# First LayerNorm's gain and offset rows made on TensorE from their columns, their load dropped and its room filled early; router logits woven between output products

## The chip, the cores and the metric

The kernel runs on one NeuronCore of one Trainium2 chip. The metric is the time of one execution on the device in microseconds (us). Three executions of the kernel before gave 1113.84, 1113.93 and 1114.98 us, so the median is 1113.93 us. A difference under 0.2% (2.2 us) counts as none here.

## What is computed

The reference is one layer of a streaming encoder in float32 for 384 tokens (a prompt of 256 and 8 streams of 16), width 1024:

```
m = W_out( concat[ beta_ret * Retention(x), beta_conv * ShortConv(x) ] )
h = LayerNorm1(alpha * x + m)            # gain ln1_g, offset ln1_b
y = LayerNorm2(alpha * h + MoE(h))       # top 4 of 32 experts, clamped SwiGLU
```

Each expert has a gate-and-up matrix of 1024 x 2048 and a down matrix of 1024 x 1024, 12 MB in all. All 32 experts are read. The router's logits are a product of h with a 1024 x 32 matrix.

## The kernel before, in words

There is one instruction stream for each engine, written out by hand, with semaphores between them. The work has two stages.

The **mixer** comes first. Its weights come in 18 pieces of 1 MB. It ends with the output products (`wout`, L793 to L809): for each of three token tiles t and eight chunks c, three matmuls of 512 columns that sum into a bank. After them come transposes of h (`transpose_h`, L811), the logits (`logits`, L820, eight chunks of 32 columns in two halves), ranks of the tokens within an expert (`ranks`, L837) and the gather of the first pair's tokens (`gather_first`, L850). The list from L867 to L902 sets their order on TensorE: `wout` of tiles 0 and 1 whole, then tile 2's last four chunks woven with the transposes and logits of tiles 0 and 1, then the rest. VectorE finishes each tile meanwhile (`residual`, `row_stats`, `logit_offset`, `choose`, called from L1688 on), and ScalarE copies transposes out of the banks and normalises rows (`copy_h_t`, `norm_rows`).

The **experts** follow, two at a time (`pair`). In TensorE's stream a pair is: `gate_up(0)`, small products, `gate_up(1)`, `down(0)`, the gather of the next pair's tokens (in the first pair it comes after `down(1)`), `down(1)`. `gate_up` has eight chunks c, each 1 MB of weights, `down` eight chunks of 0.5 MB. Both take a table of things to do between chunks. When a chunk is done, TensorE raises `piece_used`.

The weights go through rooms in SBUF: a ring of 12 rooms of 1 MB and five more (`old_rooms`), and for the first four pairs some rooms aside. Among the aside rooms is `lnp` (1 MB, called `LATE[2]` as a piece: rows of the first expert's down matrix, chunks 4 and 5 of `down(0)`). All of these DMAs are issued by SyncE, strictly in order: before an issue SyncE waits until `piece_used` says that the room's last reader is through. The queue of issues is thus stopped by the oldest room that is not yet free. In the part that matters here the order is: two pieces after the last output product, `xy` (`LATE[3]`) once `h_raw` says that VectorE's residuals are done, the two `EARLY` pieces after the last logit, two rooms as `gate_up(0)` frees them, then pair 1's pieces. Within pair 1, after its first run, SyncE waits for `h_ready` and issues `LATE[2]` into `lnp` (L525 to L527).

`lnp` is late because it holds the first norm's gain and offset until then. ScalarE issues two DMAs that spread each row of 1024 numbers over 128 partitions (L1242 to L1244, 512 KB each). VectorE multiplies and adds them to the normalised rows in `gain_and_offset` (L1625 to L1632, six operations on 128 x 1024), after its part of the first pair's gathered tokens and ahead of `softmax`. The same gain and offset are also in SBUF as columns, `ln1_t`, with 8 columns each (value p + 128 c in partition p, column c).

Further up in the mixer, `first_streams` (L743) has TensorE overwrite banks that VectorE has read in its group norm. It waits on `o_free`, raised by the last of the group norm's operations (L1525). `gate_rows(0)` (L1530) comes right behind on VectorE.

Of the kernel before, what the change touches and what calls it, by code (L numbers as in the profile page):

```python
# [29 lines left out]
ALU = mybir.AluOpType  # L30
# [3 lines left out]
D = 1024  # L34
KC = D // 128
# [94 lines left out]
def build(nc, x_tok, x_t, s_ret, conv_in, w_in, w_out, chan, beta_ret, ln1, ln2, w_router, b_router,  # L130
# [3 lines left out]
    with es:  # L134
# [121 lines left out]
        with ExitStack() as gap:  # L256
# [20 lines left out]
        xt_in, x_in, cst_in, mcst_in, st_in = map(sem, ("xt_in", "x_in", "cst_in", "mcst_in", "st_in"))  # L277
        chan_in, bias_in, ln1_in, ln2_in, router_in = map(sem, ("chan_in", "bias_in", "ln1_in", "ln2_in", "router_in"))
        rows_stored, retp_stored = sem("rows_stored"), sem("retp_stored")
# [11 lines left out]
        chan_mm, c_out, u_out, conv_ready = map(sem, ("chan_mm", "c_out", "u_out", "conv_ready"))  # L291
        gn_var, gn_rstd, o_free, o_ready_m = map(sem, ("gn_var", "gn_rstd", "o_free", "o_ready_m"))
        kd_ready, stp_mm, stp_out = sem("kd_ready"), sem("stp_mm"), sem("stp_out")
# [5 lines left out]
            sem, ("wr_ready", "wr_sum_in", "wr_sum_mm", "wr_sum_out"))  # L299
        row_shift, norm_ready, h_ready = map(sem, ("row_shift", "norm_ready", "h_ready"))  # L300
        half_gathered, first_xg, first_xg_v = map(sem, ("half_gathered", "first_xg", "first_xg_v"))
        h_t, h_t_out = sem("h_t"), sem("h_t_out")
# [110 lines left out]
        def _(sp):  # L413
# [87 lines left out]
            def aside_pieces(pair, ea, eb):  # L501

                used = MIX_PIECES + (pair - 1) * PAIR_PIECES
                aside = [run for run in runs if run[0] in LATE]
                cycled = [run for run in runs if run[0] not in LATE]
                ahead = sum(unit_of[aside_fill(pair, j) + units - 1 - WIDE] < (pair - 1) * PAIR_PIECES + LATE[0]
                            for j, units in cycled)
                for j, units in cycled[:ahead] + aside + cycled[ahead:]:
                    if j == LATE[0]:
                        sp.wait_ge(piece_used, used + LATE[0] + (1 if pair == 1 else 2))  # L510
                        if pair == 1:
                            sp.wait_ge(tab_ready, 1)
                        expert_run(j, ea, eb, over_q[:, :]).then_inc(side_again[j], 16)
                    elif j == LATE[2]:
                        k = (LATE[2] - LATE[0]) * 256
                        rows = w_down[bass.ds(ea, 1), k:k + 128 * DN_RUN, :].rearrange("e (p k) n -> p e (k n)", p=128)
                        for n, dst in ((0, last_old), (1, in_lnp)):
                            sp.wait_ge(piece_used, used + LATE[n + (1 if pair == 1 else 2)] + 1)
                            sp.dma_start(dst.unsqueeze(1), rows[:, :, n * PW:(n + 1) * PW])\
                                .then_inc(side_again[LATE[n + 2]], 16)  # L520
                    else:
                        g = aside_fill(pair, j)
                        room_used(g, units)
                        expert_run(j, ea, eb, rooms(g % WIDE, units)).then_inc(slot_full[g % WIDE], 16)
                    if pair == 1 and j == 0:  # L525
                        sp.wait_ge(h_ready, NT)
                        first_side(LATE[2])  # L527

# [53 lines left out]
            sp.wait_ge(h_raw, 2 * NT)  # L582
            first_side(LATE[3])
            sp.wait_ge(logit_mm, NT)
            for j in EARLY:
# [31 lines left out]
        def _(pe):  # L617
# [125 lines left out]
            def first_streams():  # L743

                pe.wait_ge(vm_ready, 2)
                pe.wait_ge(o_free, NT)
                pe.wait_ge(stp_out, 1)
                streams(0)
                streams(1)
# [123 lines left out]
            router_sums()  # L873
            for t in range(NT - 1):
                wout(t, range(4, KC))
            transpose_h(0, 0)
            transpose_h(0, 1)
            wout(NT - 1, (4,))
            logits(0, 0)
            wout(NT - 1, (5,))  # L880
            logits(0, 1)
            transpose_h(1, 0)
            wout(NT - 1, (6,))
            transpose_h(1, 1)
            wout(NT - 1, (7,))
            logits(1, 0)
            transpose_h(2, 0)
            logits(1, 1)
            transpose_h(2, 1)
            logits(2, 0)  # L890
            pe.wait_ge(sel_ready, 1)
            gate_up_bias(0)
            early_ranks()
# [8 lines left out]
            gather_first(2, range(KC))  # L902


            def count():
# [175 lines left out]
            def pair(turn, odd=False, last=False):  # L1081
# [14 lines left out]
                if not first:  # L1096
# [3 lines left out]
                        | ({2: lambda: sums_so_far(0), 6: lambda: sums_so_far(1)} if last else {})  # L1100
                        | ({2: count_before, 6: by_expert} if first else {}))
                pe.wait_ge(act_t_ready, 2 * p + 1)
                pe.wait_ge(sel_down_ready, p + 1)
                down(0, turn, odd, {4: lambda: transpose_act(1, p, 2 if first else DN_RUN)}
                     | ({2: overflow_tables} if first else {}) | ({6: lambda: sums_so_far(2)} if last else {}))
                if not first and not last:
# [34 lines left out]
        def _(act):  # L1141
# [99 lines left out]

            act.wait_ge(piece_used, IN_PIECES + 2)  # L1242
            for n in range(2):
                act.dma_start(lnp[:, n, :], ln1[n:n + 1, :].to_broadcast([128, D])).then_inc(ln1_in, 16)  # L1244
            act_banks = ((0, 1), (3, 7), (2, 4))
# [167 lines left out]
        def _(dve):  # L1413
# [106 lines left out]
            for t in range(NT):  # L1520
                dve.wait_ge(gn_rstd, t + 1)
                for h in range(H):
                    ins = dve.tensor_scalar(qo[:, t, h * 128:(h + 1) * 128], bank[t][:, h * 128:(h + 1) * 128],
                                            gmv[:, t, h, 0:1], grs[:, t, h:h + 1], ALU.subtract, ALU.mult)
                ins.then_inc(o_free, 1)  # L1525

            def gate_rows(t):

                dve.wait_ge(o_free, t + 1)
                dve.tensor_tensor(qo[:, t, :], qo[:, t, :], gg[:, t, :], ALU.mult).then_inc(o_ready_m, 1)  # L1530
# [93 lines left out]

            def gain_and_offset():  # L1625

                dve.wait_ge(ln1_in, 32)
                for t in range(NT):
                    ins = dve.tensor_tensor(hid[:, t, :], hid[:, t, :], lnp[:, 0, :], ALU.mult)
                link(ins)  # L1630
                for t in range(NT):
                    dve.tensor_tensor(hid[:, t, :], hid[:, t, :], lnp[:, 1, :], ALU.add).then_inc(h_ready, 1)  # L1632

# [75 lines left out]
            for c in range(4, KC):  # L1709
                dve.tensor_scalar(xg[:, c, :], bank[7][:, (c - 4) * 128:(c - 3) * 128], ln1_t[:, 0, c:c + 1],  # L1710
                                  ln1_t[:, 1, c:c + 1], ALU.mult, ALU.add).then_inc(first_xg_v, 1)
            gain_and_offset()

# [93 lines left out]
            def pair(p, first=False, second=False, last=False):  # L1807
# [8 lines left out]
                for a in range(2):  # L1816
# [13 lines left out]
                    if a == 0:  # L1830
# [4 lines left out]
                        if not last:  # L1835
                            dve.wait_ge(gt_mm, p + 1)
                            slots_of(p + 1)
                    elif not last:
                        rows_of(p + 1)
                if first:  # L1840
                    tables()
                if last:

# [100 lines left out]
```

## Time and profile before

| what | value |
|---|---|
| median of three executions | 1113.93 us |
| the profiled execution, its own time | 1113.32 us |
| its span, first to last instruction | 1111.4 us |
| TensorE busy | 97% of the span |
| DMA, hardware queue of the weights | 428.68 MB, 92.9% of 16 engines' span |
| VectorE, ScalarE, GpSimd busy | 30%, 19%, 8% |
| mean granted TensorE clock | 0.994 |

The busy time of TensorE (PE) is modelled from pipelined instructions, so it overstates how full the engine is; what counts is whether it has idle time and who ended it. A float32 matmul stands as two instructions in the trace, a float32 transpose as one. PEld is TensorE's loading of weights. SPq is SyncE's sequencer, which issues DMAs. The span leaves out 1.9 us around the profiled execution.

### The profile page before, as it was taken

The page shows a single profiled execution, that of the slowest core. Times are in us where ns is not written, and L with a number is a line of the kernel's source. Part 1 is how long each engine was busy: PE and PEld are TensorE (multiplying, and loading weights), DVE is VectorE, ACT ScalarE, POOL GpSimd, SP SyncE. Part 2 cuts the span into 40 slices and gives each one's busy share as a digit, 9 for nine tenths or more (in the row PEclk, how much of TensorE's full clock was granted, in tenths as well). Part 3 has the DMA queues.
Part 4 walks back from the last instruction along what each step waited for, and adds up shares of the span by engine and source line. Part 5 has one row for each costly group of instructions (what it writes and reads, how often), then busy time and mean ns, then how long its engine had stood idle before and what let it go on. Part 6 is the DMA issues. An engine that isn't in the chain of part 4 may idle for free.

```text
span 1111.4 us, 13640 instructions
## 1 busy us (share of the span) xinstructions
PE 1073.5 (97%) x5552; PEld 544.8 (49%) x5552; DVE 328.0 (30%) x601; ACT 207.4 (19%) x361; POOL 90.2 (8%) x50
## 2 busy tenths in 40 slices
PE   9999999999999999999999999999898989898995
PEld 6889988344434343434343434343434343342532
DVE  3487764512131312121212121212131312112134
ACT  3243333120111120202020202020111111110122
POOL 4675500000000000000000000000000000000002
PEclk9999999999999999999999999999999999999998
DMA  9972589999999999999999999999999999999995
GB/s 351 325 243 76 163 331 404 364 428 407 426 429 425 428 428 428 426 424 430 429 428 429 427 429 428 429 427 428 430 428 427 429 428 428 426 430 428 428 427 204
DMA packets 56611, 436.27 MB, mean 393 GB/s; under 512 B 8128, under 2 KB 18112, under 8 KB 29088
## 3 DMA queue, kind: packets, MB, share of 16 engines
q1 hardware_dynamic: 50048, 428.68, 92.9%
q10 hardware_dynamic: 6528, 7.09, 1.9%
q8 instruction: 26, 0.43, 0.2%
q14 instruction: 9, 0.07, 0.0%
HBM read 431.78 MB, written 3.97 MB: 392 GB/s over the span
## 4 chain that ended last, share of the span: by engine, by line
PE 67%; DMA 25%; DVE 1%; issue 0%; POOL 0%; ACT 0%; POOLq 0%; SPq 0%; DVEq 0%
PE bank L1012 25%; DMA ring<-w_down 25%; PE bank L1044 18%; PE bank L944 8%; PE bank L637 5%; PE bank L1073 1%; PE bank L993 1%; PE bank L864 1%; PE bank L1075 1%; PE bank L854 1%; PE bank L1021 1%; PE bank L800 1%; PE bank L780 1%; PE bank L786 1%; PE bank L803 1%; PE bank L804 1%
## 5 line engine op out<-in xcount | busy, mean ns | idle before, releaser
L1012 PE MATMUL bank<-ring,xg 128*64 128x512 f32 x1536 | 345.3, 595 | 7.2 <-DMA ring<-w_gu 7.1
L1012 PEld LDWEIGHTS bank<-ring,xg 128*64 128x64 f32 x1536 | 105.0, 136 | 209.1 <-issue 188.0
L1044 PE MATMUL bank<-ring,act_t 128*64 128x512 f32 x672 | 151.0, 595 | 8.3 <-DMA ring<-w_down 8.3
L1012 PE MATMUL bank<-old_rooms,xg 128*64 128x512 f32 x496 | 112.3, 595 | 3.7 <-DMA old_rooms<-w_gu 3.7
L1784 DVE SCALAR_TENSOR_TENSOR oo_lo<-oo_raw,gate_s,oo_hi 128x512 fp32r<-128x512 f32 x32 | 24.0, 752 | 311.0 <-ACT oo_hi L1288 311.0
L1820 DVE TENSOR_SCALAR gate_c<-bank 128x512 f32<-128x512 f32 x32 | 22.1, 691 | 249.8 <-PE bank L1012 249.8
L944 PEld LDWEIGHTS bank<-onehot,hid 128*128 128x128 f32 x720 | 85.9, 196 | 12.2 <-issue 12.2
L1044 PEld LDWEIGHTS bank<-ring,act_t 128*64 128x64 f32 x672 | 46.1, 137 | 92.8 <-issue 78.0
L944 PE MATMUL bank<-onehot,hid 128*128 128x128 f32 x720 | 88.8, 283 | 0.0
L1798 DVE TENSOR_TENSOR xy<-xy,bank 128x512 f32<-128x512 f32 x84 | 52.7, 683 | 107.6 <-PE bank L1075 107.6
L1380 POOL TENSOR_TENSOR rstd<-veps,minus_half 128x1 f32<-128x1 f32 x6 | 3.3, 545 | 961.7 <-DVE veps L1580 961.4
L1363 POOL TENSOR_TENSOR w_parts<-ring,w_parts 128x1024 fp32r<-128x1024 f32 x27 | 74.5, 2764 | 52.8 <-ACT w_parts L1159 52.8
L1012 PEld LDWEIGHTS bank<-old_rooms,xg 128*64 128x64 f32 x496 | 34.2, 136 | 66.7 <-issue 57.6
L1315 ACT COPY oo_raw<-bank 64x512 f32<-64x512 f32 x63 | 36.6, 581 | 159.9 <-PE bank L1044 159.1
L1044 PE MATMUL bank<-old_rooms,act_t 128*64 128x512 f32 x256 | 60.0, 609 | 3.8 <-DMA old_rooms<-w_down 3.8
L1299 ACT ACTIVATE sig<-gate_c 128x512 f32<-128x512 f32 x32 | 20.2, 630 | 177.6 <-DVE gate_c L1820 177.6
L1301 ACT COPY act_t<-bank 128x512 f32<-128x512 f32 x32 | 18.8, 586 | 167.0 <-PE bank L993 167.0
L1277 ACT CAST gt<-bank 128x384 fp32r<-128x384 f32 x16 | 7.7, 479 | 201.2 <-PE bank L956 201.2
L637 PE MATMUL bank<-w_parts,x_hi 128*128 128x512 f32 x180 | 44.8, 395 | 0.3 <-ACT w_parts L1159 0.3
L1159 ACT CAST w_parts<-ring 128x1024 fp32r<-128x1024 f32 x27 | 28.4, 1053 | 65.9 <-PE bank L637 60.3
L1073 PE MATMUL bank<-oo_hi,gt 128*128 128x512 f32 x90 | 38.6, 429 | 0.0
L637 PEld LDWEIGHTS bank<-w_parts,x_hi 128*128 128x128 f32 x180 | 33.6, 187 | 9.5 <-issue 1.5
(258 smaller groups left out, 942.9 us busy)
## 6 DMA issues: line engine op xcount, KB each, us to landing
ring<-w_gu SPq DMA_DIRECT2D x90, 2048.0 KB, 30.0
ring<-w_down SPq DMA_DIRECT2D x41, 2048.0 KB, 33.0
old_rooms<-w_gu SPq DMA_DIRECT2D x30, 2048.0 KB, 28.6
old_rooms<-w_down SPq DMA_DIRECT2D x18, 1024.0 KB, 24.8
old_rooms<-w_down SPq DMA_DIRECT2D x7, 2048.0 KB, 30.5
ring<-w_in SPq DMA_DIRECT2D x13, 1024.0 KB, 14.5
ring<-w_gu SPq DMA_DIRECT2D x12, 1024.0 KB, 6.9
over_q<-w_down SPq DMA_DIRECT2D x3, 2048.0 KB, 15.2
```

What stands on the lines that cost most here:

```text
L637: mm = pe.matmul(out, lhs, rhs, start=(n == 0 and c == 0), stop=(n == 2 and c == KC - 1))
L944: mm = pe.matmul(bank[6 + c // 4][:, (c % 4) * 128:(c % 4 + 1) * 128], hid[:, t, :].rearrange("p (q m k) -> p q k m", m=128, k=GU_RUN) [:, ...
L1012: mm = pe.matmul(bank[2 * a + n][64 * hf:64 * hf + 64, :], xg[:, c, 64 * a:64 * a + 64], w[:, col:col + 512], start=False, stop=(c == KC - 1))
L1044: mm = pe.matmul(bank[b][64 * hf:64 * hf + 64, :], act_t[:, a, c % 4, 64 * (c // 4):64 * (c // 4) + 64], w[:, c % run, hf * 512:(hf + 1) * ...
L1073: pe.matmul(bank[comb_banks[i]][:, :], gt[:, t * 128:(t + 1) * 128], oo_hi[:, hf, :], start=True, stop=False)
L1159: act.copy(w_parts[:, n % PARTS, 0, :], w).then_inc(w_hi_ready, 1)
L1299: act.activation(sig[:, :], gate_c[:, :], ACT.Sigmoid, scale=SIG).then_inc(sig_ready, 1)
L1315: act.copy(oo_raw[64 * a:64 * a + 64, hf, :], bank[down_banks[a]][64 * hf:64 * hf + 64, :]).then_inc(out_ready, 1)
L1363: pool.tensor_tensor(w_parts[:, n % PARTS, 1, :], w, w_parts[:, n % PARTS, 0, :].bitcast(F32), ALU.subtract).then_inc(w_lo_ready, 1)
L1784: dve.scalar_tensor_tensor(oo_lo[:, hf, :], oo_raw[:, hf, :], gate_s[:, 0:1], oo_hi[:, hf, :].bitcast(F32), ALU.mult, ALU.subtract).then_i ...
L1798: dve.tensor_tensor(xy[:, t, o], xy[:, t, o], bank[comb_banks[i]][:, :], ALU.add)\
L1820: dve.tensor_scalar(gate_c[:, :], bank[2 * a][:, :], LIMIT, None, ALU.min).then_inc(gate_ready, 1)
```

## The change

1. ScalarE no longer issues the two loads of the gain and offset rows. `ln1_rows(n)` on TensorE makes them: eight matmuls into banks 0 and 1, each with one column of `ln1_t`, repeated 128 times, as the stationary operand and the identity as the moving one. `ln1_rows(0)` (gain) stands before chunk 1 of the first pair's `gate_up(1)` and waits for `up_ready`; `ln1_rows(1)` (offset) stands before chunk 6 of its `down(0)` and waits until VectorE has used the gain.
2. VectorE's `gain_and_offset` becomes `rows_with`, called twice, with the banks as the second operand: the gain after `slots_of(1)` in the first pair, the offset after `tables`.
3. `LATE[2]` is issued right behind `LATE[3]`; the wait for `h_ready` inside pair 1 goes.
4. The order of the output products, transposes and logits is woven tighter.
5. `o_free` goes; `first_streams` waits for the first `gate_rows` instead.

```diff
-                    if pair == 1 and j == 0:
-                        sp.wait_ge(h_ready, NT)
-                        first_side(LATE[2])
...
             sp.wait_ge(h_raw, 2 * NT)
             first_side(LATE[3])
+            first_side(LATE[2])
             sp.wait_ge(logit_mm, NT)
...
-                pe.wait_ge(o_free, NT)
+                pe.wait_ge(o_ready_m, 1)
...
             router_sums()
-            for t in range(NT - 1):
-                wout(t, range(4, KC))
+            wout(0, range(4, KC))
             transpose_h(0, 0)
+            wout(1, (4, 5))
             transpose_h(0, 1)
-            wout(NT - 1, (4,))
+            wout(1, (6,))
             logits(0, 0)
-            wout(NT - 1, (5,))
+            wout(1, (7,))
             logits(0, 1)
+            wout(2, (4,))
             transpose_h(1, 0)
-            wout(NT - 1, (6,))
+            wout(2, (5,))
             transpose_h(1, 1)
-            wout(NT - 1, (7,))
+            wout(2, (6,))
             logits(1, 0)
+            wout(2, (7,))
+            logits(1, 1)
             transpose_h(2, 0)
-            logits(1, 1)
+            pe.wait_ge(sel_ready, 1)
+            gate_up_bias(0)
             transpose_h(2, 1)
             logits(2, 0)
-            pe.wait_ge(sel_ready, 1)
-            gate_up_bias(0)
             early_ranks()
             logits(2, 1)
...
+            def ln1_rows(n):
+
+                if n == 0:
+                    pe.wait_ge(up_ready, 1)
+                else:
+                    pe.wait_ge(ln1_used, NT)
+                for c in range(KC):
+                    mm = pe.matmul(bank[c // 4][:, (c % 4) * 128:(c % 4 + 1) * 128],
+                                   ln1_t[:, n, c:c + 1].to_broadcast([128, 128]), ident, start=True, stop=True)
+                mm.then_inc(ln1_mm, 1)
...
-                        | ({2: count_before, 6: by_expert} if first else {}))
+                        | ({1: lambda: ln1_rows(0), 2: count_before, 6: by_expert} if first else {}))
...
-                     | ({2: overflow_tables} if first else {}) | ({6: lambda: sums_so_far(2)} if last else {}))
+                     | ({2: overflow_tables, 6: lambda: ln1_rows(1)} if first else {}) | ({6: lambda: sums_so_far(2)} if last else {}))
...
-            act.wait_ge(piece_used, IN_PIECES + 2)
-            for n in range(2):
-                act.dma_start(lnp[:, n, :], ln1[n:n + 1, :].to_broadcast([128, D])).then_inc(ln1_in, 16)
...
-                ins.then_inc(o_free, 1)
+            link(ins)
...
-            def gain_and_offset():
-
-                dve.wait_ge(ln1_in, 32)
+            def rows_with(n, op, done):
+
+                dve.wait_ge(ln1_mm, n + 1)
                 for t in range(NT):
-                    ins = dve.tensor_tensor(hid[:, t, :], hid[:, t, :], lnp[:, 0, :], ALU.mult)
-                link(ins)
-                for t in range(NT):
-                    dve.tensor_tensor(hid[:, t, :], hid[:, t, :], lnp[:, 1, :], ALU.add).then_inc(h_ready, 1)
+                    dve.tensor_tensor(hid[:, t, :].rearrange("p (b n) -> p b n", b=2),
+                                      hid[:, t, :].rearrange("p (b n) -> p b n", b=2), banks[:, 0:2, :], op)\
+                        .then_inc(done, 1)
...
-            gain_and_offset()
...
+                        if first:
+                            rows_with(0, ALU.mult, ln1_used)
...
                 if first:
                     tables()
+                    dve.wait_ge(ln1_used, NT)
+                    rows_with(1, ALU.add, h_ready)
```

## Rows read from the trace of the kernel before

**Rows 1.** The page: busy time by engine, and what the DMAs moved in 40 slices

```profile
PE 1073.5 (97%) x5552; PEld 544.8 (49%) x5552; DVE 328.0 (30%) x601; ACT 207.4 (19%) x361; POOL 90.2 (8%) x50
...
GB/s 351 325 243 76 163 331 404 364 428 407 426 429 425 428 428 428 426 424 430 429 428 429 427 429 428 429 427 428 430 428 427 429 428 428 426 430 428 428 427 204
```

**Rows 2.** Busy time by stretch: from:to length, engines, clock, DMA share, GB/s

```profile
194.00:198.00 4.00, 4.00 (x21) 1.43 (x22) 3.82 (x7) 0.78 (x3) 0.00 (x0) 1.00 0.34 94
...
254.50:256.50 2.00, 2.00 (x12) 0.65 (x10) 0.00 (x0) 0.00 (x0) 0.00 (x0) 1.00 0.92 279
256.50:300.00 43.50, 43.50 (x231) 20.20 (x229) 9.92 (x18) 5.45 (x11) 0.00 (x0) 1.00 1.00 424
...
640.00:1090.00 450.00, 426.92 (x2152) 181.49 (x2154) 92.61 (x158) 63.80 (x118) 0.00 (x0) 1.00 1.01 428
```

**Rows 3.** SyncE's queue in order of time: start, us, what is issued

```profile
186.41 0.80 SPq L479 DMA_DIRECT2D early_rooms<-w_gu  x2
...
202.50 0.33 SPq L483 DMA_DIRECT2D lnp<-w_down  x1
...
254.66 3.76 SPq L494 DMA_DIRECT2D ring<-w_down  x2
```

**Rows 4.** What SyncE's queue waited for, 186 to 256 us: total, times, longest

```profile
SPq L494 <- PE bank L1012: 9.5, 1, 9.5
```

**Rows 5.** TensorE in order of time, pair 1's start and a late pair

```profile
251.01 7.04 PE L1012 MATMUL bank<-ring,xg 128*64 128x512 f32 x32
257.97 0.50 PE L1073 MATMUL bank<-oo_hi,gt 128*128 128x512 f32 x1
...
667.20 3.65 PE L1044 MATMUL bank<-old_rooms,act_t 128*64 128x512 f32 x16 [0.73 <-DMA old_rooms<-w_down]
```

**Rows 6.** TensorE: the first full gather, and eight transposes

```profile
244.70 5.92 PE L944 MATMUL bank<-onehot,hid 128*128 128x128 f32 x48
...
173.81 1.03 PE L814 MATMUL bank<-cst,hid 128*128 128x128 f32 x8
```

**Rows 7.** DMA issues by line: KB each, median us to landing

```profile
lnp<-ln ACTq DMA_DIRECT2D x4, 512.0 KB, 6.8
```

**Rows 8.** VectorE in order of time, first pair; idle before it in brackets

```profile
208.60 0.68 DVE L1821 TENSOR_SCALAR up_c<-bank 128x512 f32<-128x512 f32 x1
...
225.83 0.69 DVE L1820 TENSOR_SCALAR gate_c<-bank 128x512 f32<-128x512 f32 x1 [9.27 <-PE bank L1012]
...
246.29 0.75 DVE L1784 SCALAR_TENSOR_TENSOR oo_lo<-oo_raw,gate_s,oo_hi 128x512 fp32r<-128x512 f32 x1 [15.85 <-ACT oo_hi L1288]
```

**Rows 9.** The page's groups: a VectorE operation that reads a bank

```profile
L1798 DVE TENSOR_TENSOR xy<-xy,bank 128x512 f32<-128x512 f32 x84 | 52.7, 683 | 107.6 <-PE bank L1075 107.6
```

**Rows 10.** In order of time: the first gate_rows on VectorE, first streams on TensorE

```profile
115.79 2.22 DVE L1530 TENSOR_TENSOR qo<-qo,gg 128x512 f32<-128x512 f32 x1
...
117.99 1.15 PE L739 MATMUL bank<-tmp,kk 32*128 32x256 f32 x16
```

**Rows 11.** TensorE in order of time, from the ranks to the first gate_up

```profile
184.38 0.41 PE L841 MATMUL bank<-vv,cst 128*128 128x32 f32 x2 [0.22 <-DVE vv L1649]
...
186.19 4.55 PE L854 MATMUL bank<-onehot,hid 128*128 128x128 f32 x26
...
191.16 2.90 PE L854 MATMUL bank<-onehot,hid 128*128 128x128 f32 x22
```

**Rows 12.** By stretch: TensorE's clock is the third number from the end

```profile
230.10:233.50 3.40, 3.40 (x9) 0.63 (x6) 0.35 (x3) 0.00 (x0) 0.00 (x0) 0.50 1.04 443
182.30:185.70 3.40, 3.18 (x29) 2.66 (x27) 2.55 (x14) 2.87 (x5) 0.51 (x1) 1.00 1.00 407
185.70:189.10 3.40, 3.40 (x17) 3.40 (x17) 2.15 (x11) 2.57 (x5) 0.00 (x0) 0.50 1.04 439
```

**Rows 13.** TensorE in order of time, down(0) of the first pair

```profile
229.89 3.53 PE L1044 MATMUL bank<-old_rooms,act_t 128*64 128x512 f32 x8
...
234.03 1.94 PE L1044 MATMUL bank<-lnp,act_t 128*64 128x512 f32 x8
```

More of the change, by code:

```diff
@@ L277, in build @@
         xt_in, x_in, cst_in, mcst_in, st_in = map(sem, ("xt_in", "x_in", "cst_in", "mcst_in", "st_in"))
-        chan_in, bias_in, ln1_in, ln2_in, router_in = map(sem, ("chan_in", "bias_in", "ln1_in", "ln2_in", "router_in"))
+        chan_in, bias_in, ln2_in, router_in = map(sem, ("chan_in", "bias_in", "ln2_in", "router_in"))
         rows_stored, retp_stored = sem("rows_stored"), sem("retp_stored")
@@ L291, in build @@
         chan_mm, c_out, u_out, conv_ready = map(sem, ("chan_mm", "c_out", "u_out", "conv_ready"))
-        gn_var, gn_rstd, o_free, o_ready_m = map(sem, ("gn_var", "gn_rstd", "o_free", "o_ready_m"))
+        gn_var, gn_rstd, o_ready_m = map(sem, ("gn_var", "gn_rstd", "o_ready_m"))
         kd_ready, stp_mm, stp_out = sem("kd_ready"), sem("stp_mm"), sem("stp_out")
@@ L300, in build @@
         row_shift, norm_ready, h_ready = map(sem, ("row_shift", "norm_ready", "h_ready"))
+        ln1_mm, ln1_used = sem("ln1_mm"), sem("ln1_used")
         half_gathered, first_xg, first_xg_v = map(sem, ("half_gathered", "first_xg", "first_xg_v"))
@@ L1524, in _ @@
                                             gmv[:, t, h, 0:1], grs[:, t, h:h + 1], ALU.subtract, ALU.mult)
-                ins.then_inc(o_free, 1)
+            link(ins)
             def gate_rows(t):
-                dve.wait_ge(o_free, t + 1)
                 dve.tensor_tensor(qo[:, t, :], qo[:, t, :], gg[:, t, :], ALU.mult).then_inc(o_ready_m, 1)
```

## The prediction, made before the changed kernel was run

> **What bounds the kernel now.** I read the page first. TensorE is busy 97% of the span, and in the slices the DMAs move about 428 GB/s from some 170 us on, almost to the end [rows 1]. Two resources are nearly full, so I asked in which stretch each sets the pace.
>
> The table of stretches answers. From 640 to 1090 us the DMAs carry 428 GB/s without a pause, while TensorE has 23 us of idle time in 450 [rows 2]. The order of time shows what ends that idle time: a landing of expert weights [rows 5]. So the stream of weights sets the end. It runs without a gap from 256.5 us on: 424 GB/s up to 300, and the slices show no dip after that [rows 1, 2].
>
> What matters is therefore when the stream last had a gap, and who ended it. Between 254.5 and 256.5 us it moved only 279 GB/s [rows 2]. SyncE's queue issued the next transfer at 254.66 us [rows 3], after a wait of 9.5 us for TensorE's line 1012 [rows 4]. That line is the first `gate_up` of pair 1, 32 instructions from 251.01 us, four chunks [rows 5]. Two of them take half of 7 us, which gives 254.5. All rooms were full, and TensorE had to free one. **From there on the stream follows TensorE's progress at 254.66 us**, and what lies behind is the same number of bytes at the same rate. An earlier gap, 194 to 198 us at 94 GB/s [rows 2], is of the same kind and is made good by the later one: whatever the stream gains or loses before 254.66 us only changes how long it stands there.
>
> TensorE has no idle time from 186 us to 254.66 us, and 0.22 us just before that stretch [rows 11]. So the end moves with the sum of TensorE's work and waits up to 254.66 us. The one limit is the gap's own length: at 279 in place of 428 GB/s over 2 us the stream lost 0.7 us there. If TensorE came earlier by more than that, plus what the DMAs gain, the stream would be the limit.
>
> **Bytes.** The two removed loads are 512 KB each [rows 7], 1.05 MB together, and at 428 GB/s worth 2.45 us of stream. `LATE[2]`, issued at 202.50 us before [rows 3], moves about 20 us earlier, behind `LATE[3]`; its 1.05 MB now go ahead of the gap at 194 us, for which TensorE has to free nothing. The `EARLY` pieces behind it in the queue (issued at 186.41 us [rows 3]) land up to 2.45 us later, at about 198 us, since the stream's gap at 194 us says that all had landed by then. They are chunks 6 and 7 of `gate_up(0)`, which begins at 194 us behind the first gather [rows 11]; six chunks of 1.75 us [rows 5] make 204 us: nobody waits. The wait for `h_ready` goes from SyncE's queue, and with it at most the few tenths by which `LATE[2]` followed the piece before it. All this puts the stream 2.45 us ahead at 254.66 us. It stands still there 2.45 us longer. Value: 0.
>
> **New matmuls.** `ln1_rows` is called twice, eight matmuls each, 16 float32 matmuls of 128 columns with 128 columns of weights, so 32 instructions. The nearest row is a gather with the same shapes: 48 instructions from 244.70 us, 5.92 us, 0.122 us each [rows 6]. I take 32 x 0.122 = **3.9 us**. Nothing hides them: TensorE is in order and has no idle time there. From below, eight transposes of the same tile size took 1.03 us, 0.13 us each with one instruction each [rows 6]; if a matmul with a repeated column cost no more than one of these, 16 would be 2.1 us. From above, 0.132 us an instruction as in the 22 of the first gather [rows 11], which gives 4.2 us. That the column is repeated by a step of zero has no row; I see no reason for a gain or a loss in it.
>
> The Trainium skill, "Perfetto Trace Analysis", section "Optimizing Tensor Performance", asks that a logical transpose be made as a transpose and not as a standard matmul. The trace agrees: one instruction in place of two [rows 6]. By it the new rows would cost 2.1 us and not 3.9, but the change uses the matmul.
>
> **Waits that the new matmuls bring to TensorE.** `ln1_rows(0)` waits for `up_ready`, raised by an operation of 0.68 us from 208.60 us [rows 8], so at 209.3 us. It stands one chunk of 1.75 us into `gate_up(1)`, and `gate_up(0)` was through by 208 us, when VectorE began to read its banks; so TensorE is there at 209.8 us at the earliest, with small products between the two later: no wait. `ln1_rows(1)` waits until VectorE has used the gain. An operation that reads a bank takes 0.683 us for 512 columns [rows 9], so one of 1024 takes 1.37 and three take 4.1 us. They fall into 9.27 us in which VectorE had nothing to do before 225.83 us [rows 8]. The call comes at chunk 6 of `down(0)`, about 236 us before the shift [rows 13]: no wait. The offset is again 4.1 us on VectorE, in idle time of 15.85 us [rows 8]. It has to be through when the gather begins, at 244.70 us before [rows 6], some 8.7 us after chunk 6. That leaves 4.6 us. If this cover went, the gather would stand still for what is over. `gain_and_offset` leaves VectorE's queue ahead of `softmax`; TensorE waited for nothing of it, so this is worth 0.
>
> **`first_streams`.** The new wait ends with `gate_rows(0)`, which ran from 115.79 us for 2.22 us, to 118.01; TensorE started at 117.99 us [rows 10]. The extra link on VectorE adds about a tenth. I take 0.2 us on TensorE; the bounds are 0 and 0.4.
>
> **The woven order.** No product is added or taken away between the mixer's end and `gate_up(0)`. The last output product comes one half of logits later, so SyncE's pieces behind it are issued 1 us later; that only moves a stall of the stream ahead of 194 us. What can be won on TensorE is the 0.22 us of waiting before the ranks [rows 11], and something of its clock. I take 0.2 us off.
>
> **The clock.** Twice before 254.66 us the granted clock is 0.50, so 1.2 instead of 2.4 GHz: from 185.7 to 189.1 us and from 230.1 to 233.5 us [rows 12]. Before the first, TensorE ran 29 short instructions with 0.22 us of idle time [rows 12]; the change puts one more half of transposes into that time and takes the idle time out. In the first, 26 gather instructions took 4.55 us, 0.175 each, against 0.132 for the 22 after it [rows 11]: 1.1 us. In the second, eight instructions took 3.53 against 1.94 us [rows 13]: 1.6 us. Neither has to stay where it was, and a shift of the work may bring another. Bounds: 2.7 us less, 1.6 us more. The first is the one that the woven order works against; I take half of it, 0.6 us less.
>
> **The sum.** 3.9 + 0.2 - 0.2 - 0.6 = 3.3 us later at 254.66 us, and as much later at the end. On the profiled execution's 1113.3 us that makes 1116.6; its own time was 0.6 us under the median of three, so against the median it is 1113.9 + 3.3 = **1117.2 us**.
>
> **Rivals.**
>
> *The stream's bytes decide, not its last gap.* This is the only way to a faster kernel that I see. The stream is 2.45 us shorter, and if it were not TensorE that lets it run at 254.66 us, all of that would be seen: 1111.5 us. For it: the DMAs are the fuller of the two resources behind 640 us. Against it: the wait of 9.5 us [rows 4], right where the rate falls. It decides if TensorE gets to 254.66 us earlier than now, and with 3.9 us of new work that takes a gain of 4 us elsewhere. In "Perfetto Trace Analysis", section "Identifying the Most-Contended Engine", the Trainium skill says to optimise the engine with the highest utilisation first; by that the removed bytes are the gain, and this rival is what that rule would give here. Chance 0.07.
>
> *Both stretches at half clock vanish.* 3.9 + 0.2 - 0.2 - 2.7 = 1.2 us: 1115.1 us, which is no change by the bound of 0.2% (2.2 us), about what a measurement of this kernel can tell from none. With it goes the case that the new matmuls are as cheap as transposes (2.1 in place of 3.9 us, 1.8 us less than the forecast, 1115.4 us). Chance 0.24.
>
> *Another half-clock stretch, or a wait for VectorE.* 1.6 us more than without any gain of clock: 3.9 + 1.6 = 5.5 us, 1119.4 us. A late offset, where VectorE would hold the gather by a microsecond, ends about there too. Chance 0.11.
>
> **How the numbers follow.** My forecast has 0.58; its own range is 1116.0 to 1118.3 us. The range goes down to the case of a better clock and up to the third rival: 1114.7 to 1119.4 us. Slower by over 0.2% (above 1116.2 us) hold nearly all of the forecast, 0.53, and the third rival: 0.64. Within 0.2%: the rest of the forecast and the second rival, 0.29. Faster: 0.07.
>
> **What would show it.** In the changed profile, two groups of 16 matmul instructions of 128 columns at the new line, 1.9 to 2.1 us each, with no idle time before them; the first `gate_up` of pair 1 starts at about 254.3 instead of 251.0 us; the stream has a deeper gap ahead of its issue, now near 258 us, about 3 us longer than before; 428 GB/s after it; and `rows_with` ends some 4 us before the gather. If the gap before pair 2's first down piece is gone, or that issue comes earlier than 254.66 us, my account is wrong; if it comes 1 us later only, the clock has been kinder than I took it to be.

## The result, and the profile after

The changed kernel takes **1118.2 us** (median of 8, 1115.26 to 1119.16), the kernel before 1114.95 us (median of 8, 1112.47 to 1115.63). The ratio is 1.003 [1.002, 1.004], which is 3.3 us slower; forecast were 3.3 us more and slower by over 0.2%. The mean granted clock differs between executions of one kernel, mostly from 0.992 to 0.997, and those with the higher clock are shorter by up to some 3 us, which matters below. The median of before was 1.0 us higher than in the first three runs, so the time itself is 1.0 us above the forecast of 1117.2, inside the range.

The profiled execution of the changed kernel took 1115.26 us, the shortest of its eight, with a span of 1113.2 us. The page shows 32 more TensorE instructions and 288 fewer packets in ScalarE's queue q10, which had 6528, against [rows 1]:

```profile
PE 1074.9 (97%) x5584; PEld 546.7 (49%) x5584; DVE 327.9 (29%) x601; ACT 207.6 (19%) x361; POOL 90.2 (8%) x50
...
GB/s 350 323 244 78 161 336 358 364 424 391 425 429 428 427 427 427 427 425 429 428 428 429 426 429 428 429 427 429 429 428 428 427 430 426 428 428 429 427 427 205
...
q10 hardware_dynamic: 6240, 6.04, 1.6%
```

The table of stretches, with the columns of [rows 2]:

```profile
212.50:216.00 3.50, 3.50 (x20) 1.29 (x20) 0.94 (x7) 0.00 (x0) 0.00 (x0) 1.00 0.41 80
255.50:258.50 3.00, 3.00 (x18) 0.98 (x16) 0.00 (x0) 0.00 (x0) 0.00 (x0) 1.00 0.60 147
258.50:300.00 41.50, 41.50 (x221) 19.50 (x219) 9.91 (x18) 4.89 (x11) 0.00 (x0) 1.00 1.00 423
640.00:1090.00 450.00, 426.99 (x2153) 181.35 (x2150) 92.57 (x158) 62.65 (x116) 0.00 (x0) 1.00 1.01 428
```

The last gap is deeper, 147 GB/s over 3 us against 279 over 2, and the rate behind it is unchanged. The earlier gap of [rows 2], at 194 us, now stands at 212.5 us. SyncE's queue in order of time, and below it what the queue waited for between 186 and 260 us:

```profile
182.53 0.65 SPq L484 DMA_DIRECT2D lnp<-w_down  x1
...
256.49 3.76 SPq L495 DMA_DIRECT2D ring<-w_down  x2
```

```profile
SPq L495 <- PE bank L1024: 12.6, 2, 9.5
```

`LATE[2]` leaves at 182.53 instead of 202.50 us, and the issue that ends the last gap is at 256.49 instead of 254.66 us [rows 3], behind a wait for the same first `gate_up` of pair 1 (line 1024 is line 1012 of before). That is 1.83 us later, and the span is 1.8 us longer. TensorE in order of time:

```profile
185.07 0.41 PE L840 MATMUL bank<-vv,cst 128*128 128x32 f32 x2 [0.65 <-DVE vv L1656]
186.77 3.17 PE L853 MATMUL bank<-onehot,hid 128*128 128x128 f32 x26
...
210.59 2.05 PE L913 MATMUL bank<-cst,ln_t 128*128 128x128 f32 x16
...
231.19 1.94 PE L1056 MATMUL bank<-old_rooms,act_t 128*64 128x512 f32 x8
...
235.60 2.05 PE L913 MATMUL bank<-cst,ln_t 128*128 128x128 f32 x16
...
246.54 5.92 PE L956 MATMUL bank<-onehot,hid 128*128 128x128 f32 x48
252.84 7.04 PE L1024 MATMUL bank<-ring,xg 128*64 128x512 f32 x32
```

Line 913 is `ln1_rows`: two groups of 16, 2.05 us each, with no wait. The first gather's 26 instructions take 3.17 us where they took 4.55 [rows 11], and in the first pair's `down(0)` the eight that read `old_rooms` take 1.94 us where the same eight had taken 3.53 [rows 13]. No group stands at 1.2 GHz any more: both stretches of [rows 12] are gone in this execution. VectorE in order of time, the lines of `rows_with`:

```profile
217.78 3.46 DVE L1637 TENSOR_TENSOR hid<-hid,bank 128x1024 f32<-128x1024 f32 x3
...
237.79 3.48 DVE L1637 TENSOR_TENSOR hid<-hid,bank 128x1024 f32<-128x1024 f32 x3 [6.04 <-PE bank L913]
```

The gain is through at 221.2 us and the offset at 241.3, 5.3 us before the second gather.

The granted clock of this execution was 0.997 on the mean; the other seven had 0.993 to 0.996. The two profiles therefore compare an execution with 1.2 GHz in two stretches (before) with one without any. What the change costs at the same clock is not in this pair, and it took runs of parts to see it.

### The profile page after: what moved, and what is told of

Its sections match the earlier page's. It is cut to its first block, busy times and chain, and to the rows that moved or that the text cites. A ratio compares the mean times of both kernels' runs of the same rounds, so it can differ in the third digit from the quotient of the medians.

```text
span 1113.2 us, 13702 instructions
## 1 busy us (share of the span) xinstructions
PE 1074.9 (97%) x5584; PEld 546.7 (49%) x5584; DVE 327.9 (29%) x601; ACT 207.6 (19%) x361; POOL 90.2 (8%) x50
## 4 chain that ended last, share of the span: by engine, by line
PE 67%; DMA 25%; DVE 1%; issue 0%; POOL 0%; ACT 0%; POOLq 0%; SPq 0%; DVEq 0%
PE bank L1024 25%; DMA ring<-w_down 25%; PE bank L1056 18%; PE bank L956 8%; PE bank L636 5%; PE bank L1085 1%; PE bank L1005 1%; PE bank L863 1%; PE bank L1087 1%; PE bank L1033 1%; PE bank L799 1%; PE bank L853 1%; PE bank L779 1%; PE bank L785 1%; PE bank L802 1%; PE bank L803 1%
```

## Experiments

e1 to e4 share 35 runs of the kernel before (median 1115.04 us), e5 to e8 share 33 (1114.11), e9 and e10 share 22 (1114.74). A difference in us that stands beside a ratio is worked out from the ratio; the medians themselves differ a little otherwise, by up to 1.1 us. Beside the medians I read one number from each trace: when SyncE issued the first down piece of pair 2, the issue that follows the last gap.

**e1: before, plus the products alone**

```diff
+            def dummy_rows(n):
+
+                if n == 0:
+                    pe.wait_ge(up_ready, 1)
+                for c in range(KC):
+                    pe.matmul(bank[c // 4][:, (c % 4) * 128:(c % 4 + 1) * 128],
+                              ln1_t[:, n, c:c + 1].to_broadcast([128, 128]), ident, start=True, stop=True)
...
+                        | ({1: lambda: dummy_rows(0), 2: count_before, 6: by_expert} if first else {}))
...
+                     | ({2: overflow_tables, 6: lambda: dummy_rows(1)} if first else {}) | ({6: lambda: sums_so_far(2)} if last else {}))
```

> The kernel before with nothing changed but 16 more matmuls on TensorE, of the form and at the two places of ln1_rows, their results used by nobody. If TensorE's work up to the first gate_up of pair 1 sets the end, the time rises by 32 instructions of 0.122 to 0.128 us, 3.9 to 4.1 us, and the first gate_up of pair 1 starts that much later. If the bytes of the stream set it, the time stays (within 0.7 us), since no byte is moved more or less. Mean granted clock about 0.994 to 0.997 in both.

1117.63 us (12 runs), ratio 1.0027 [1.0015, 1.0039], 3.0 us slower. TensorE and, below, SyncE's queue:

```profile
211.62 2.05 PE L910 MATMUL bank<-cst,ln_t 128*128 128x128 f32 x16
...
236.62 2.05 PE L910 MATMUL bank<-cst,ln_t 128*128 128x128 f32 x16
```

```profile
257.51 3.76 SPq L494 DMA_DIRECT2D ring<-w_down  x2
```

The products alone, without early rooms or fewer bytes, cost as much as the whole change (3.0 and 3.3 us, with about 1.3 us either way).

**e2: before, without the two loads**

```diff
-            act.wait_ge(piece_used, IN_PIECES + 2)
-            for n in range(2):
-                act.dma_start(lnp[:, n, :], ln1[n:n + 1, :].to_broadcast([128, D])).then_inc(ln1_in, 16)
...
-                dve.wait_ge(ln1_in, 32)
...
-                    ins = dve.tensor_tensor(hid[:, t, :], hid[:, t, :], lnp[:, 0, :], ALU.mult)
+                    ins = dve.tensor_tensor(hid[:, t, :], hid[:, t, :], hid[:, t, :], ALU.mult)
...
-                    dve.tensor_tensor(hid[:, t, :], hid[:, t, :], lnp[:, 1, :], ALU.add).then_inc(h_ready, 1)
+                    dve.tensor_tensor(hid[:, t, :], hid[:, t, :], hid[:, t, :], ALU.add).then_inc(h_ready, 1)
```

> The kernel before without the two loads of the first norm's gain and offset rows (1.05 MB less); VectorE's six operations stay and take the rows themselves as second operand, so the hidden rows are multiplied by themselves and doubled instead of scaled and offset. If TensorE's progress sets the end: no change, within 0.5 us, and the stream has a longer gap ahead of 194 us. If the bytes set it: 2.45 us faster.

1114.49 us (11 runs), ratio 0.9996 [0.9985, 1.0007]: 0.5 us less, with at most 1.7 us inside the interval. The 2.45 us of "the bytes decide" are ruled out. The profiled execution had no half-clock stretch before 262 us, issued at 251.74 us, and its stream had no gap there; this row covers the place:

```profile
245.00:262.00 17.00, 17.00 (x91) 8.52 (x90) 3.34 (x6) 1.08 (x2) 0.00 (x0) 1.00 1.01 424
```

e1 has in the same stretch:

```profile
245.00:262.00 17.00, 17.00 (x103) 9.71 (x100) 1.91 (x3) 3.77 (x6) 0.00 (x0) 1.00 0.93 362
```

In that execution of e2 the last gap is the one at 194 us (115 GB/s from 194 to 196 us), and the removed bytes lie ahead of it too.

**e3: before, with the woven order alone**

```diff
-            for t in range(NT - 1):
-                wout(t, range(4, KC))
+            wout(0, range(4, KC))
             transpose_h(0, 0)
+            wout(1, (4, 5))
...
-            transpose_h(2, 1)
-            logits(2, 0)
             pe.wait_ge(sel_ready, 1)
             gate_up_bias(0)
+            transpose_h(2, 1)
+            logits(2, 0)
             early_ranks()
```

> The kernel before with the new order of output products, transposes, logits and bias products alone. No work is added. If TensorE sets the end: between 0.0 and 1.3 us faster, by the waiting ahead of the ranks and by the half-clock stretch around 186 us where it goes away; I expect 0.8. In the changed kernel's trace that stretch was absent and the wait ahead of the ranks longer (0.65 us), so the first gate_up should start 0 to 0.8 us earlier. If the bytes set it: no change.

1115.98 us (11 runs), ratio 1.0009 [0.9997, 1.0021]: 1.0 us more. A gain was expected, and the medians do not show it. TensorE's first rank products:

```profile
185.13 0.41 PE L841 MATMUL bank<-vv,cst 128*128 128x32 f32 x2 [0.66 <-DVE vv L1651]
```

The wait ahead of the ranks is 0.66 us here, 0.65 in the changed kernel and 0.22 before [rows 11]. All twelve kernels do the same work on TensorE from the start of the first streams (117.99 us before [rows 10]) to that of the first `gate_up`; only its order differs. The times between these two marks in the twelve traces, in us:

```text
kernels                 order  between          1.2 GHz in it
e2, e8, e10             old    74.51 to 74.53   none
after, e3, e4, e5       new    75.19 to 75.20   none
before, e1, e9          old    76.00 to 76.16   3.4 us
e6                      old    77.65            6.8 us
e7                      new    78.31            6.8 us
```

The new order costs TensorE 0.67 us at the same clock. It makes that up only when the half-clock stretch goes with it. The stretch at 186 us stands in one profile of the five with the new order (e7; not in after, e3, e4, e5) and in four of the seven with the old one (before, e1, e6, e9). With one profile each, it stays open whether the order is the cause.

**e4: after, with two products instead of 16**

```diff
-                for c in range(KC):
+                for c in (KC - 1,):
```

> The changed kernel with only the last of the eight matmuls in each call of ln1_rows, so 14 matmuls (28 instructions) fewer; the other seven blocks of the gain and offset rows are whatever stands in the banks. If TensorE sets the end: 28 x 0.124 = 3.5 us faster than the changed kernel, so about the time of the kernel before, 0.2 us less. If something else in the change costs the time (the early load, VectorE reading banks): it stays near the changed kernel, 3.3 us above before.

1116.92 us (11 runs), ratio 1.0016 [1.0001, 1.0031]: 1.9 us, where nearly nothing was expected. The trace shows why. Each group of two instructions still takes 0.49 us, where 2 x 0.124 was expected.

```profile
210.75 0.49 PE L913 MATMUL bank<-cst,ln_t 128*128 128x128 f32 x2
```

From the first `gate_up` to that of pair 1 it needs 56.52 us, against 55.42 in e2 and e8, which have no product and no half clock there. So 1.1 us are left of the products; the new order adds its 0.67, which makes 1.8.

**e5: after, with transposes instead of matmuls**

```diff
-                    mm = pe.matmul(bank[c // 4][:, (c % 4) * 128:(c % 4 + 1) * 128],
-                                   ln1_t[:, n, c:c + 1].to_broadcast([128, 128]), ident, start=True, stop=True)
+                    mm = pe.transpose(bank[c // 4][:, (c % 4) * 128:(c % 4 + 1) * 128],
+                                      ln1_t[:, n, c:c + 1].to_broadcast([128, 128]), ident)
```

> The changed kernel with ln1_rows made of transposes (one instruction each) in place of matmuls with the identity (two each). If TensorE's work sets the end: 32 x 0.124 = 4.0 us become 16 x 0.10 to 0.13 = 1.6 to 2.1 us, so 1.9 to 2.4 us faster than the changed kernel, 1.1 us above the kernel before. If the number of instructions doesn't matter: as the changed kernel, 3.3 us above before.

1116.06 us (12 runs), ratio 1.0027 [1.0011, 1.0043], 3.0 us (the medians are 1.95 apart). Its time does not tell it from the changed kernel. The trace does:

```profile
210.58 1.09 PE L913 MATMUL bank<-cst,ln_t 128*128 128x128 f32 x8
...
234.63 1.09 PE L913 MATMUL bank<-cst,ln_t 128*128 128x128 f32 x8
```

The way between the two `gate_up` is 57.72 us, 2.3 above e2 where the products add 4.2. The issue is at 254.55 us, 1.9 earlier than in the changed kernel. That this lead reaches the end is not shown. Its four executions at a granted clock of 0.997 took 1115.05 to 1115.47 us, and the five of after, e6 and e7 at that clock 1115.05 to 1116.06.

**e6: after, with the old order.** The edit is e3's in reverse.

> The changed kernel with the order of output products, transposes and logits of the kernel before. If the woven order gives TensorE something: 0.2 to 1.3 us slower than the changed kernel, so 3.5 to 4.6 us above before. If it gives nothing: 3.3 us above before.

1117.97 us (12 runs), ratio 1.0031 [1.0017, 1.0045]: 3.5 us. In the medians the new order neither makes nor saves the loss; the 0.67 us of e3's table is too little to show in them.

**e7: after, with `LATE[2]` at its old place and no wait**

```diff
+                    if pair == 1 and j == 0:
+                        first_side(LATE[2])
...
             first_side(LATE[3])
-            first_side(LATE[2])
```

> The changed kernel with the room lnp called for its expert piece where the kernel before had it, behind pair 1's first run, but without a wait. If the stream stands still ahead of pair 1's refill until TensorE frees a room, moving 1.05 MB within the time before that is worth nothing: as the changed kernel, 3.3 us above before. If the early call is a gain that the new products hide: 2.45 us slower than the changed kernel, 5.7 us above before.

1118.33 us (10 runs), ratio 1.0034 [1.002, 1.0049]: 3.8 us. The early room gives nothing that shows, and costs nothing either.

**e8: before, with 1.05 MB more behind the gap.** The same two loads are issued once more, by SyncE, well behind pair 2's first down piece.

```diff
...
+            for n in range(2):
+                sp.dma_start(lnp[:, n, :], ln1[n:n + 1, :].to_broadcast([128, D])).then_inc(extra_in, 16)
...
+                        act.wait_ge(extra_in, 32)
```

> The kernel before with 1.05 MB more to load behind the last gap of the stream: after the issues of pair 5 SyncE loads the gain and offset rows once more into lnp, which nobody reads. Behind the gap every byte counts if the stream sets the end there: 2.45 us slower than before. If TensorE has the last word there too: no change.

1116.65 us (12 runs), ratio 1.0022 [1.0009, 1.0034]: 2.5 us, the price of 1.05 MB at 428 GB/s. With e2 this is the clearest pair: the same bytes are worth 0.5 us, or nothing, ahead of the last gap and 2.5 us behind it. The late pairs show where it is seen, TensorE waiting longer for its last ring piece (in the kernel before the same wait was 0.57 us):

```profile
1085.38 1.94 PE L1047 MATMUL bank<-ring,act_t 128*64 128x512 f32 x8 [2.10 <-DMA ring<-w_down]
```

**e9 and e10: less TensorE work before the gap.** e9 is the kernel before without most of the overflow tables' products and transposes; e10 is the changed kernel with the old order, the same work left out, and one product of 8 columns in each `ln1_rows`.

```diff
-                for t in range(NT):
-                    pe.transpose(bank[6][0:E, t * 128:(t + 1) * 128], rank_all[:, t, 0:E], ident)
-                for t in range(NT):
+                for t in (NT - 1,):
...
-                for t in range(NT):
-                    o = slice(t * OV, (t + 1) * OV)
-                    pe.matmul(bank[6][:, o], tr[:, 0, t * 128:(t + 1) * 128], oh, start=True, stop=False)
-                    pe.matmul(bank[6][:, o], ones[0:E, :], off, start=False, stop=True)
-                    pe.matmul(bank[7][:, o], tr[:, 1, t * 128:(t + 1) * 128], oh, start=True, stop=True)
```

> The kernel before without 18 of the 20 instructions of the overflow tables and without five of the six transposes ahead of them (about 2.6 us of TensorE's work in the first pair; the ranks and gates of overflow blocks are left as they stand in the banks). If TensorE's pace at pair 1's refill sets the end only as long as it is the slower one, the gain stops where the stream no longer stands still: in the traces the end less the spread of the last landings was 1107.6 us before and 1104.9 in the two runs without a gap at 254 us, so 2.0 to 2.8 us faster than before, and no gap of the stream behind 205 us. If TensorE alone sets it: 2.6 us and up to 1.6 more, up to 4.2 us faster, with the gap still there.

> The changed kernel with the old order, the same work left out as in the run beside it, and ln1_rows reduced to one product of 8 columns per call (the gain and offset rows are what stands in the banks): the early room and the absent load alone, with TensorE out of the way. If the 1.05 MB that now go ahead of the last gap count once TensorE is no longer late, it is 1.5 to 2.5 us faster than the run beside it, 4 to 5 us faster than before. If the early room is worth nothing whatever TensorE does: the same as the run beside it.

e9: 1113.23 us (12 runs), ratio 0.9992 [0.9982, 1.0002], 0.9 us faster, less than expected, and its interval includes no change. e10: 1112.33 us (10 runs), ratio 0.9984 [0.9974, 0.9994], 1.8 us faster and also about half of what was expected; the intervals of the two overlap. Their stretches, e9 first:

```profile
205.00:245.00 40.00, 40.00 (x215) 17.11 (x211) 10.90 (x37) 9.59 (x17) 0.00 (x0) 1.00 1.00 422
245.00:262.00 17.00, 17.00 (x90) 8.07 (x90) 3.76 (x6) 1.00 (x3) 0.00 (x0) 1.00 1.02 429
```

```profile
205.00:245.00 40.00, 40.00 (x216) 17.49 (x213) 17.32 (x39) 9.59 (x17) 0.00 (x0) 1.00 0.97 404
245.00:262.00 17.00, 17.00 (x87) 7.89 (x88) 3.77 (x6) 1.25 (x4) 0.00 (x0) 1.00 1.01 426
```

In e9 the stream has no gap left: it is now the limit, and TensorE's issue at 250.46 us, 4.2 us earlier than before, brings the point at which 355 MB are still to land only from 267.56 to 266.53 us. The 2.0 to 2.8 us expected of e9 came from e2 and e8, in which the stretch at 186 us is absent too: there the gap at 194 us ended at 194.65 and 194.25 us, in the kernel before at 195.97 and in e9 at 196.03.

In e10 that point is at 264.63 us, 1.9 us earlier still with TensorE's issue 0.3 us earlier. But e10's execution had no half clock and e9's had the stretch at 186 us, and TensorE ended the gap at 194 us 1.2 us earlier in e10 (194.85 us). That leaves at most 0.7 us for the bytes and the early room. The five executions of e10 at a granted clock of 0.997 took 1111.27 to 1111.93 us, and nine of the kernel before at that clock 1110.85 to 1112.01. So a gain from the bytes or the early room is not shown by e10. Part of it would be lost in a gap near 213 us (404 GB/s over 40 us), which in e10 is the last one.

## Why the prediction was right

**What sets the end: right.** Four executions side by side, times in us from the span's start; the last column is span less issue less the spread of the last 2 MB ring transfer (see the last section).

```text
kernel   1st gate_up  pair 1's  issue    355 MB left  span     spread  rest
before   193.99       251.01    254.66   267.56       1111.36  3.75    852.95
after    193.20       252.84    256.49   269.31       1113.17  3.66    853.02
e1       194.23       253.87    257.51   270.22       1113.95  3.30    853.14
e5       193.19       250.91    254.55   267.48       1112.93  5.03    853.35
```

In these, and in e3, e4, e6 and e7, the rest is 852.9 to 853.4 us: the end follows the issue one to one. e9 shows the limit: there it is 855.4. The prediction said that TensorE could come 0.7 us earlier before the stream would be the bound; measured from e9 it is 1.0 us (267.56 less 266.53).

That holds only for a lead won between the two gaps. TensorE ends the gap at 194 us as well, so a lead won ahead of that one moves the stream too. e2 shows it. TensorE issues 2.9 us earlier there than in the kernel before, the 355 MB are left at 264.89 us, 2.7 us earlier, and the rest is 853.2. The prediction took the earlier gap for one that the later one makes good. That is so for a delay, but for a gain it was the earlier gap that decided how much of it lasts.

**The bytes: right.** Worth 0 within the interval in e2 and in e7 against the changed kernel, 2.5 us when behind the gap (e8). The Trainium skill, "Perfetto Trace Analysis", section "Identifying the Most-Contended Engine", says to optimise the most contended engine first. By that rule the removed loads should have been the gain. e2 does not agree: they lie ahead of a gap that TensorE ends.

**The matmuls: right place, 0.3 too little.** 3.9 us forecast, 4.1 in the two groups, 4.22 between the two `gate_up` (59.64 less 55.42). The value lies at the upper bound: 0.128 us an instruction in the groups and 0.132 by the way between the two `gate_up`, rather than 0.122.

**No waits on `ln1_rows` and `rows_with`: right.** Line 913 has no idle time ahead. VectorE needed 3.5 us, not 4.1, for three operations of 1024 columns.

**`first_streams`, +0.2: right place, 0.1 too much.** TensorE's first streams start 1.49 to 1.50 us after the start of the group ahead of them in the traces with the old wait, and 1.61 to 1.62 us after it in those with the new one.

**The woven order, -0.2: the wrong step.** I read the 0.22 us of waiting as time that the order could win. The order brings TensorE to the ranks before VectorE has them, so the wait is 0.65 us, and the first `gate_up` is 0.67 us later at the same clock (e3).

**The clock, -0.6: chance in the profile, open over all executions.** In the profiled execution both stretches went, as the second rival had it: 4.22 of products less 1.6 for the second stretch less 0.8 at the first `gate_up` is 1.8 us, just what the issue and the span moved. That rival's 1115.1 us met the profiled execution's 1115.26, but that is one execution of eight. The kernel before has such executions too. Four profiles have a mean clock of 0.997, and none of them has a stretch (after, e2, e5, e10), so I take an execution at 0.997 for one without. Nine of the kernel before at 0.997 took 1110.85 to 1112.01 us, median 1111.5. The changed kernel has one, 1115.26; with those of e6 and e7 there are five, 1115.05 to 1116.06, median 1115.3. That is 3.8 us more. At 0.994 or less the medians are 1115.2 (59 executions of the kernel before) and 1118.5 (17 of after, e1, e6 and e7), 3.3 us more. So the profiles' 1.8 us come from comparing different clocks, and at like clock the change costs 3.3 to 3.8 us. That the new work gains some clock may still be: 59 of 90 executions before had 0.994 or less, and 17 of 42 of after, e1, e6 and e7. It was not tested.

**The sum: met in part by luck.** On TensorE the parts at the same clock are 4.22 + 0.12 + 0.67 = 5.0 us, where the prediction had 3.9 + 0.2 - 0.2 = 3.9. The median moved by 3.3 us, as forecast, so 1.7 us were taken back where 0.6 were forecast. Of these, 0.25 us is the stream's (e2); the clock may have given some, and the spread of the landings was 1.0 us smaller in the changed kernel than in e2. How much each of the two last gave is not shown. By the prediction's own signs the changed profile lies between its two cases: the issue came 1.8 us later, not 3 and not 1.

**The rivals.** "Bytes decide" fell with e2. A second wait for VectorE did not appear. Another half-clock stretch did, in e6 and e7, which had one of 6.8 us near 186 us and issued at 259.12 and 259.65 us; that belongs to single executions, as their medians do not stand out.

## What to carry to other kernels

Look for the last gap of a long transfer stream and who ends it: work on that engine ahead of that point costs its time (here 4.2 us on TensorE), bytes ahead of it cost nothing as long as the gap remains, and bytes behind it cost their time (2.5 us per 1.05 MB). A lead won there beyond the gap's own length lasts only as far as it brings the gap before that one forward too. Before two profiles are compared, see that they have the same granted clock: here the profiles are 1.8 us apart, and executions at like clock 3.3 to 3.8. For parts of 1 us and less, measure the way between two marks on the engine in the traces: it gave 0.67 us for the order within 0.02 us, where medians of 12 runs leave 1.3 us either way. Such a number is the engine's, and it need not reach the end, as e5 shows.

## What was not expected

**The 16 DMA engines drift apart.** Each engine reports its share of a transfer. The first and the last of the 16 reports of one 2 MB transfer are 0.5 us apart at 200 us in the kernel before and 3.75 at its end; at the end of the others it is 3.3 (e1) to 7.0 us (e9). The last gap brings it back to 0.7 us (262 us in the kernel before). By 279 us it is at 2.3 again, and from there it grows in single steps; in these kernels they are of 1.2 to 1.7 us (before at 467 us, after at 440, e3 at 325 and 516) and stays within about 0.2 us between them. The slowest engine's piece releases TensorE, so this spread adds to the end: e5 has its issue 0.1 us before that of the kernel before and a span 1.6 us longer, and its spread is 1.3 us larger. The steps fall within about 2 us of packets of 16 KB in the instruction queue, each of about 1 us. Most such packets bring no step, though: the kernel before has ten between 298 and 519 us, and one step. That they are the cause was not tested.

**Half clock comes and goes in the same kernel.** Up to pair 1's first `gate_up` the traces show 1.2 GHz for 3.4 us twice before [rows 12], once in e1, e3 and e9, for 6.8 us in e6 and e7, and never in after, e2, e4, e5, e8 and e10. Nothing in the kernels explains which, since e2 and before issue the same TensorE work. One stretch of 3.4 us is worth 1.5 to 1.6 us, as much as several of the parts measured here.

**A repeated column is no dearer, and a transpose is half the price.** The stationary operand with a step of zero takes 2.05 us for 16 instructions, 0.128 each, between the 0.123 and 0.132 of the gathers [rows 6, 11]; as transposes the eight columns take 1.09 us. The rule on logical transposes that the prediction quoted from the Trainium skill ("Perfetto Trace Analysis", section "Optimizing Tensor Performance") is borne out on TensorE by e5's trace: 2.3 us in place of 4.2. A gain in e5's time is not shown.
